# Eight row buffers and a ninth place that keeps weight tiles, in a kernel of attention, experts and product-key lookup

## The reference, cut to what matters

```python
def short_conv_mixer(xn, w_in, conv_w, w_out):
    bg, cg, hx = jnp.split(xn @ w_in, 3, axis=-1)
    u = cg * hx
    y = causal_depthwise_conv(u, conv_w)          # 3 taps
    return (bg * y) @ w_out

def peer(xn, w_q, sub_keys, u, v):
    q = (t @ w_q).reshape(n_tok, 8, 2, 128)       # 8 heads, two halves
    sc = einsum('thpd,hpnd->thpn', q, sub_keys)   # 128 keys a half
    # top 16 of each half, top 16 of their 256 sums: expert rows eidx, softmax gate
    hid = gelu(einsum('td,thkd->thk', t, u[eidx]))
    return einsum('thk,thkd->td', gate * hid, v[eidx])
```

## Time and profile before

| | us |
|---|---|
| median of 3 runs | 2231.38 (2229.43 to 2231.91) |
| the profiled execution | 2230.41 |
| its span, first to last instruction | 2228.6 |
| busy: PE / DVE / POOL / ACT | 1831.3 / 1307.7 / 672.5 / 484.9 |
| moved by DMA | 768.82 MB, of which 542.37 on the gathers' queue |

### The profile page before, as it was taken

How to read it: one execution, slowest core, us unless ns; L and a number is a source line. 1 busy time by engine, 2 the same in 40 slices (tenths; PEclk the granted TensorE clock), 3 DMA queues, 4 the chain that set the end, 5 groups by cost and what they waited for, 6 DMA issues and landing times.

```text
span 2228.6 us, 18733 instructions
## 1 busy us (share of the span) xinstructions
PE 1831.3 (82%) x5744; PEld 875.8 (39%) x5744; DVE 1307.7 (59%) x3325; ACT 484.9 (22%) x1214; POOL 672.5 (30%) x593
## 2 busy tenths in 40 slices
PE   8999996988779969888768877768888777878875
PEld 4445554332234635344223323324343433434332
DVE  1343424111123356767777978897677798777764
ACT  1232321111101222222221212222121222222221
POOL 1110001110000024434444434444333445444442
PEclk9999996999989989999999988889999988999999
DMA  6432237999773199999999999999999999999995
GB/s 239 167 118 104 102 130 315 413 417 418 304 291 137 54 381 371 422 420 421 421 421 422 384 422 419 421 421 421 413 421 421 384 422 414 420 422 421 421 420 243
DMA packets 112295, 768.82 MB, mean 345 GB/s; under 512 B 15856, under 2 KB 16544, under 8 KB 20416
## 3 DMA queue, kind: packets, MB, share of 16 engines
q0 software_dynamic: 78928, 542.37, 59.2%
q1 hardware_dynamic: 30672, 215.17, 24.3%
q10 hardware_dynamic: 2592, 10.04, 1.2%
HBM read 769.62 MB, written 10.49 MB: 350 GB/s over the span
## 4 chain that ended last, share of the span: by engine, by line
DMA 31%; DVE 17%; PE 10%; issue 10%; POOL 4%; ACT 1%; POOLq 0%; DVEq 0%; ACTq 0%
DMA arena<-in_c_rows_dram,arena 31%; DVE arena L2509 7%; POOL arena L2577 4%; PE banks L308 4%; PE banks L2169 2%; DVE x L2519 2%; PE banks L2495 1%; PE banks L1796 1%; DVE arena L2440 1%; DVE arena L2402 1%; DVE arena L2405 1%; PE banks L339 1%; DVE arena L2444 1%; PE banks L354 1%; DVE arena L2411 1%
## 5 line engine op out<-in xcount | busy, mean ns | idle before, releaser
L2495 PE MATMUL banks<-arena 128*128 128x512 f32 x1792 | 891.4, 644 | 274.7 <-ACT arena L2559 269.7
L2577 POOL DMA_INDIRECT arena<-in_c_rows_dram,arena x512 | 594.2, 1161 | 819.1 <-PE banks L2495 540.2
L2509 DVE CUSTOM_DVE_ANT_0 arena<-arena,xn 128x1024 f32<-128x1024 f32 x512 | 624.6, 1222 | 261.3 <-DMA arena<-in_c_rows_dram,arena 259.9
L2495 PEld LDWEIGHTS banks<-arena 128*128 128x128 f32 x1792 | 349.7, 204 | 762.7 <-ACT arena L2559 370.5
L308 PE MATMUL banks<-ring,hT 128*128 128x512 f32 (+1 forms) x672 | 284.3, 579 | 0.0
L2559 ACT ACTIVATE arena<-ident,small 128x128 f32<-128x128 f32 x448 | 158.8, 395 | 542.5 <-DVE small L2516 525.3
L308 PEld LDWEIGHTS banks<-ring,hT 128*128 128x128 f32 x672 | 123.5, 190 | 141.1 <-issue 139.0
L360 ACT COPY arena<-banks 128x512 f32<-128x512 f32 (+4 forms) x211 | 97.2, 488 | 323.5 <-PE banks L354 125.1
L2550 ACT ACTIVATE small<-small 128x2 f32<-128x2 f32 x256 | 52.2, 204 | 493.7 <-DVE small L2509 493.6
L386 POOL TENSOR_TENSOR small<-small 128x1 f32<-128x1 f32 (+4 forms) x24 | 34.2, 1423 | 360.7 <-DVE small L382 358.8
L365 DVE COPY arena<-banks 128x512 f32<-128x512 f32 (+1 forms) x45 | 30.5, 680 | 134.1 <-PE banks L1332 71.9
(11 more groups left out here) (297 smaller groups left out, 1592.4 us busy)
## 6 DMA issues: line engine op xcount, KB each, us to landing
arena<-in_c_experts_dram SPq DMA_DIRECT2D x53, 1024.0 KB, 27.1
ring<-in_c_experts_dram SPq DMA_DIRECT2D x33, 1024.0 KB, 27.5
ring<-in_c_w_in_dram SPq DMA_DIRECT2D x30, 1024.0 KB, 4.8
ring<-in_c_odd_w_in_dram SPq DMA_DIRECT2D x21, 1024.0 KB, 9.4
ring<-in_c_w_q_dram SPq DMA_DIRECT2D x20, 1024.0 KB, 9.1
ring<-in_c_even_w_in_dram SPq DMA_DIRECT2D x14, 1024.0 KB, 5.5
arena<-in_c_rows_dram,arena POOLq DMA_INDIRECT x512, 13.8
ring<-in_c_odd_w_out_dram SPq DMA_DIRECT2D x8, 1024.0 KB, 9.7
```

The costliest lines, as they stand in the source:

```text
L2495: r = e.matmul(banks[:, bank_of[("acc", L, c, hf)], :], diag[:, diag_of[m], :], rows[:, m % NB, D + hf * 512:D + (hf + 1) * 512], start=fi ...
L2509: e.tensor_tensor_reduce(u, u, xn[:, c, :], 1.0, 0.0, ALU.mult, ALU.add, hid3[:, c, h, k:k + 1]).then_inc(ve.sem, ve.up(("u", p)))
L2577: e.indirect_dma_start(rows[:, b, :], None, table_uv, bass.IndirectOffsetOnAxis(ap=eix[:, c, 16 * h + k:16 * h + k + 1], axis=0)).then_inc ...
```

## The change: what it does

`NB` goes from 9 to 8. The memory of the ninth buffer becomes `kept_tile`, a seventh place for weight tiles (number NSLOT = 6), which `load` and `tile` reach through `place_of`. `KEPT` gets a fourth tile, hx,1,0, in that place, and in chunk 1's order `OB[1]` the factors hx and cg of the first half change places, so that its first four tiles are the kept ones. `KEPT_Q` gets a fifth head, 3, in slot 4, and head 5 moves to the new place. For chunk 0, head 3's product, scores and choice go 4 positions later (`late`). Which of two factors goes through ACT and which through DVE is now said by their order (`factor`). The ring narrows to three slots one load earlier.

```diff
--- before.py
+++ after.py
@@ -18,7 +18,7 @@
 D = 1024
 NSLOT = 6
-NB = 9
+NB = 8
 NDIAG = 6
 AHEAD = 5
 AR = 28672
@@ -272,13 +272,17 @@
             s, before = rings.next_slot(name, place)
             if before is not None:
                 e.wait_ge(*spent[before])
-            e.dma_start(ring[:, s, 0:src.shape[1]], src).then_inc(landed[s].sem, landed[s].up(name, by=16))
+            e.dma_start(place_of(s)[:, 0:src.shape[1]], src).then_inc(landed[s].sem, landed[s].up(name, by=16))
+
+        def place_of(s):
+
+            return ring[:, s, :] if s < NSLOT else kept_tile
         def tile(e, name, n):
             s = slot_of[name]
             e.wait_ge(landed[s].sem, landed[s].at(name))
-            return ring[:, s, :] if n == 0 else ring[:, s, :].rearrange("p (k c) -> p k c", k=n)
+            return place_of(s) if n == 0 else place_of(s).rearrange("p (k c) -> p k c", k=n)
         def used(name):
             spent[name] = (pe.sem, pe.n)
@@ -2033,6 +2037,7 @@
         at[0] = 0
         rows = place(NB * 2 * D).rearrange("p (i d) -> p i d", i=NB)
+        kept_tile = place(2048)
         qp = [place(512) for _ in range(2)]
         sc0 = [place(256) for _ in range(2)]
         sc1 = [place(256) for _ in range(8)]
@@ -2069,12 +2074,19 @@
 
         OB = ((("cg", 0), ("hx", 0), ("bg", 0), ("cg", 1), ("hx", 1), ("bg", 1)),
-              (("bg", 1), ("cg", 1), ("hx", 1), ("cg", 0), ("hx", 0), ("bg", 0)))
+              (("bg", 1), ("hx", 1), ("cg", 1), ("cg", 0), ("hx", 0), ("bg", 0)))
         part_at = {(c, *part): j for c in range(2) for j, part in enumerate(OB[c])}
-
-        KEPT = {("hx", 1, 4): 3, ("bg", 1, 0): 4, ("bg", 1, 4): 5}
-        KEPT_Q = {4: 4, 5: 5, 6: 3, 7: None}
+        def factor(c, j):
+
+            kind, hf = OB[c][j]
+            if kind == "bg":
+                return 0
+            return 1 if j == min(part_at[c, "cg", hf], part_at[c, "hx", hf]) else 2
+
+
+        KEPT = {("hx", 1, 0): NSLOT, ("hx", 1, 4): 3, ("bg", 1, 0): 4, ("bg", 1, 4): 5}
+        KEPT_Q = {3: 4, 4: 5, 5: NSLOT, 6: 3, 7: None}
         def odd_tile(c, j, k):
             part = (*OB[c][j], k)
@@ -2130,8 +2142,9 @@
             norm_steps(base + 76, "ffn21", c)
             put(base + 79, "turn", "ffn21", c)
             for i, h in enumerate(HEADS[1, c]):
-                head_steps(base + (81, 91)[i] if i < 2 else base + SEG + 16 * (i - 2) - 2, c, h)
-                choices_at[base + (100, 112)[i] if i < 2 else base + SEG + 16 * (i - 2) + 8] = (1, c, h, 3)
+                late = 4 if (c, h) == (0, 3) else 0
+                head_steps(base + (81, 91)[i] if i < 2 else base + SEG + 16 * (i - 2) - 2 + late, c, h)
+                choices_at[base + (100, 112)[i] if i < 2 else base + SEG + 16 * (i - 2) + 8 + late] = (1, c, h, 3)
         put(2 * SEG + 20, "gain", "fin", "mix1")
         norm_steps(3 * SEG + 4, "fin", 0)
@@ -2145,7 +2158,7 @@
                         part, hf = OB[c][j]
                         kept = KEPT.get((part, hf, k))
                         if kept is None or c == 0:
-                            if kept == 3:
+                            if kept == NSLOT:
                                 rings.narrow(3)
                             load(e, odd_tile(c, j, k), w_odd[(OCOL[part] + 512 * hf) // 256 + k // 4], kept)
                     if what[0] == "out" and what[3] % 4 == 0:
@@ -2235,7 +2248,7 @@
                     rings.drop(name)
             if kind == "turn_u":
                 _, c, hf = what
-                e.wait_ge(ve.sem, ve.at(("O", c, part_at[c, "hx", hf])))
+                e.wait_ge(ve.sem, ve.at(("u", c, hf)))
                 turn(e, ("uT", c, hf), [ub[:, 512 * hf + i * P:512 * hf + (i + 1) * P] for i in range(4)])
             if kind == "turn_b":
                 _, c, hf = what
@@ -2310,7 +2323,7 @@
             if kind == "in" and what[3] == 7:
                 _, c, j, _ = what
                 kind_, hf = OB[c][j]
-                if kind_ != "hx":
+                if factor(c, j) != 2:
                     dst = bgb if kind_ == "bg" else ub[:, 512 * hf:512 * hf + 512]
                     act_unload(e, ("O", c, j), dst, banks[:, bank_of[("O", c, j)], :])
             if kind == "turn_u":
@@ -2349,13 +2362,13 @@
                     e.tensor_copy(uT[:, :, 0:2], uT[:, :, 128:130]).then_inc(ve.sem, ve.up(("edge", c)))
                 else:
                     e.memset(uT[:, :, 0:2], 0.0).then_inc(ve.sem, ve.up(("edge", c)))
-            if kind == "in" and what[3] == 7 and OB[what[1]][what[2]][0] == "hx":
+            if kind == "in" and what[3] == 7 and factor(what[1], what[2]) == 2:
                 _, c, j, _ = what
                 name, hf = ("O", c, j), OB[c][j][1]
                 u = ub[:, 512 * hf:512 * hf + 512]
                 e.wait_ge(ac.sem, ac.at(("O", c, j - 1)))
                 e.wait_ge(pe.sem, pe.at(name))
-                e.tensor_tensor(u, u, banks[:, bank_of[name], :], ALU.mult).then_inc(ve.sem, ve.up(name))
+                e.tensor_tensor(u, u, banks[:, bank_of[name], :], ALU.mult).then_inc(ve.sem, ve.up(name, ("u", c, hf)))
                 emptied[name] = (ve.sem, ve.n)
             if kind == "conv":
                 _, c, k = what
```

## The result

The changed kernel takes **2236.94 us** (median of 8 runs, 2233.90 to 2240.59) against 2231.39 us in 8 runs of the kernel before on the same chip (2229.43 to 2232.69). The medians differ by 5.6 us. The ratio that is on record with the runs is 1.0022, 95% interval 1.0013 to 1.0031: 4.9 us slower, between 2.9 and 6.9. The profiled execution took 2234.65 us, 4.2 more than that of before.

What follows compares the result with a forecast made beforehand. The prediction took DMA's gathers, a full belt at about 421 GB/s from 886 us, to bound the kernel. Its terms, -5.0 + 2.5 + 1.2 + 2.1 = +0.8 us, gave 2232.2 us, no change, range 2227.5 to 2238.

Steps and rivals of the forecast that it cites:

- rival B: Belt runs dry at seven thin spots, 877 to 1766 us, a whole row each: 2243.8 us; chance 0.19.
- Bytes: Full belt: one odd_w_in and one w_q load fewer, 2 x 2.49, so 5.0 us less.
- First stretch: 809 to 886 us, belt already dry behind PE: everything after comes one row late, +2.5 us.
- Head-score blocks: First chunk, PE's 7 us product every 16 rows: asks after 961, 1003 and 1046 us cost +1.2 us.
- DVE's full stretch: 1240 to 1260 us, conv and a head's choice together: the shortest ask sets the cost, +2.1 us.
- Asks that take over 8.8 us are harmless: Buffer rule for the whole stage: asks landing later than 8.8 us cost nothing with one buffer fewer.
- 1766 us: Next DVE-held place, at 1765.7 us: its ask took 9.0 us, so cost 0, high end 1.2.
- SP's order: Second pass: reordered loads and head 3's later steps make nothing late, 0 us, high end 2.5.
- rival C: Near 1562 us: head 3's late tile holds PE and the belt, +2.5, 2234.7 us; chance 0.08.
- one buffer fewer: Gather m waits for row m-8's use, not m-9's; costs only where the belt runs thin: 2.5 + 1.2 + 2.1.
- Rival A: Buffer is free, eight in flight suffice everywhere, the two tiles pay whole: 2226.4 us; chance of faster 0.10.
- the sum of -2.3: Alternative total using the skill page's 4.4 us gather time, closing thin spots after 886 us: -5.0 + 2.5 + 0.2.

Runs made afterwards that it cites:

- nb8_only: Kernel before with eight row buffers instead of nine, loads and order unchanged: 2243.41 us, ratio 1.0050, +11.2 us.
- ask4_nb8: Changed kernel with AHEAD 4 in place of 5: 2237.16 us, ratio 1.0022 to the kernel before.
- choice_nb8: Changed kernel with the DVE choice beside the conv at 1240 us begun five positions earlier, four steps a position: 2235.34 us, 1.0013 to the kernel before.
- order_only: Kernel before, nine buffers and three kept tiles, with the changed second-pass order and head 3 four positions later: 2230.83 us, ratio 0.9996.
- depth3: Kernel before, nine buffers, each ask waiting for DVE's row m - 3, so at most two gathers ahead; AHEAD 2: 2478.54 us, ratio 1.1109.
- depth4: Kernel before, nine buffers, each ask waiting for DVE's row m - 4, so at most three gathers ahead; AHEAD 3: 2263.83 us, ratio 1.0143.
- spread_nb8: Changed kernel with layer-0 products of heads 3 to 7 in eight parts over eight positions: 2235.47 us, ratio 1.0022 to the kernel before.
- the two best kernels: Same hold-shortening edits on the changed kernel (eight buffers), 2230.60 us, and on the kernel before (nine), 2230.57 us.
- best_nb8: Changed kernel with AHEAD 4, head products spread, one choice moved off the conv, turn and first two head products later: 2230.60 us, 0.9993 to before.

## Why the prediction was right and where it was wrong

The forecast said no change and a time in 2227.5 to 2238 us, and the time lies there; that is in part luck. It is above the high end of the sum (2235.7) and inside the range only because this was stretched towards rival B. The mechanism was right in its signs and in two of its places, and one term, the buffer, was too small by about half.

- *Bytes, -5.0 us.* Right: the counts are 20 and 19, and alone they give -4.7 [-6.7, -2.7].
- *First stretch, one row, +2.5.* Right within what can be read: 3.0 in nb8_only, 1.3 to 3.2 in three others with eight buffers; in the kernel after the shift against before grows by 2.4 us up to row 29 (a start 1.0 us earlier included).
- *Head-score blocks, +1.2.* The step that failed: "the hole is 6.3 - (latency of n - 2.48)". nb8_only shows 3.2 there, above the high end of 2.7, ask4_nb8 2.9 and choice_nb8 3.3; the kernel after has 1.9. So 1.2 was too low, by 1 to 2 us.
- *DVE's full stretch, +2.1.* Right: 2.3 in nb8_only between rows 163 and 183, 2.4 in the kernel after.
- *"Asks that take over 8.8 us are harmless."* Wrong, the largest miss: 3.7 us between 1347 and 1527 us in nb8_only, where asks had taken 9.1 to 10.0 us; 1.1 in the kernel after, which then loses 2.4 more up to its end. *"From 1300 on still 421 GB/s"* is refuted by 391 and 408 GB/s at 1380 to 1420 us.
- *1766 us, 0, high end 1.2.* 1.1 in nb8_only between rows 330 and 345, at the high end.
- *SP's order, 0.* Right as far as the runs tell: order_only, which has the new order but not the kept tiles, has -0.9 [-2.9, +1.1]. PE's wait at 1580.2 is gone, and no wait appears near 1562 us (rival C).
- *Signs that were named.* The counts of loads, POOL's longer wait and the median landing (11.2 us in nb8_only) came as written. "The stretch up to 886 us with less DMA" did not: 834 to 854 us has 308 GB/s after and 299 in the earlier trace rows.
- *Readings.* 421 GB/s begins with the seventeenth slice of the earlier trace rows; the sixteenth has 371. The wait of 9.6 us at 961.5, given to PE, has DVE's L2509 as releaser in the earlier trace rows. Neither enters the sum.

The timeline of PE, kernel after: the first product of head 3, which waits for nothing.

```profile
1563.37 0.61 PE L2285 MATMUL banks<-hT,ring 128*128 128x128 f32 x4
```

The term "one buffer fewer" was 5.8 and measured 11.2 [8.0, 14.3]. Two things had been read wrongly. The latency on a nearly dry belt was taken from 5.8 and 6.3 us, yet it is no constant: in nb8_only the asks of that kind take 5.5 to 7.6 us. And two gathers ahead were taken as a full belt, since the rows of 8.2 and 8.5 us fit such a sum. depth3 and depth4 contradict this: with two ahead all along an ask costs 0.51 us, with three 0.07.

Rival B (dry at every thin spot, a whole row each) had the sign, and its lower end, 2236.3, is near the time. Its mechanism isn't what happened: of its seven places none but 877 us and 1250 us costs about a whole row, the four blocks from 918 to 1046 cost 3.2 together instead of 9.9, and much of the rest is lost at a place it does not list. Rival A (the buffer is free) is refuted by nb8_only; so is the sum of -2.3 that followed from the Trainium skill's "DMA: Bandwidth & Descriptors", section "Anatomy of one DMA — SWDGE (gpsimd) path": its fit, by which 4.4 us was the estimate for such a gather, is below every one of the landings, the shortest of which, in the kernels read here, is 5.3.

Open: why the kernel after loses about 2.4 us after 1527 us by its landings, and nb8_only 0.7. The loads, in which the two differ, do not explain it: ask4_nb8, choice_nb8 and spread_nb8 have the loads of the kernel after and lose nothing there (0.0, -1.1 and -1.3 us by the same count), so it may be no more than the difference of one execution from another. That eight and nine buffers end level in the two best kernels is shown; that best_nb8's remaining 16 thin asks are what offsets its two tiles is only argued (it has five such asks more than before, 2.6 us at 0.51, and saves 5.0 by the tiles: -2.4, and one to three us for the first stretch, where -1.6 [-3.6, +0.4] was measured).

## What to carry to other kernels

A buffer less takes one transfer from the depth of the queue at *every* ask: count the asks that have three or fewer transfers ahead now, and price them with a kernel that caps the depth. One such run showed here what a rule from two latencies had missed. The result is an upper estimate: in the trace of before 39 asks from row 30 on have three or fewer ahead and 11 of them two, so 28 x 0.51 = 14.3 us, and with 2.5 for the first stretch 16.8, where 11.2 was measured; the rule had said 5.8. Where a tile's load is traded for a buffer (2.5 us a load here), first shorten the longest holds of the engines that free buffers: four edits of this kind together turned +4.9 us into about -1.6 [-3.6, +0.4]. And a gap between two gathers' landings is not idle DMA: what else was asked for may have filled it.

## What the runs showed of the hardware

- Two 1 MB gathers ahead of an ask do not keep the DMA engines at full rate: 353 GB/s in depth3 against 417 at the usual depth; three ahead give 406 in depth4.
- POOL's gather instruction takes 0.94 us at its shortest, and 1.7 to 2.0 us at places where DVE is busy with a head's choice (1400.33 to 1404.73 us in nb8_only). That the two go together is seen, not why.
- Times of one kernel spread more with eight buffers: 6.4 to 11.2 us from the fastest to the slowest of 7 to 12 runs in five kernels (4.1 in the 5 runs of nb8_only), against 3.3 to 5.8 us in 11 runs of each with nine. The kernel before has 6.3 in 23 runs, so this is a hint and not more.
